# The recurrent half of the output projection as seven half-size products for eight, added to x in DRAM

## The reference, cut to what matters

```
merged = concatenate([rmsnorm(o, attn_out_g), rmsnorm(y_lru, lru_out_g)], -1)   # 512 + 512 columns
h = x + merged @ w_out                                                          # w_out 1024 x 1024
f = square(relu(rmsnorm(h, norm_mlp_g) @ w_up)) @ w_down
return h + f
```

## Time and profile before

| | us |
|---|---|
| executions, least / median / most | 2460.33 / 2461.35 / 2462.65 |
| span of the profiled execution | 2460.3 |
| TensorE busy in it | 2447.1 (99%) |
| VectorE / ScalarE / GpSimd busy | 1782.1 / 1250.7 / 517.4 |
| recurrent half of the projection, layer 0 | about 458.6 to 506.7 |
| attention half of it, layer 0 | about 506.7 to 554.4 |

### The profile page before, as it was taken

The page is one execution under the profiler, slowest core; times in us unless marked ns, Lnnn a source line. Parts: engine busy times, 40 slices in busy tenths (PEclk is TensorE's granted clock), DMA queues, the critical chain, the costliest instruction groups (busy, mean ns, idle before and its releaser), DMA issues.

```text
span 2460.3 us, 43868 instructions
## 1 busy us (share of the span) xinstructions
PE 2447.1 (99%) x17366; PEld 2361.9 (96%) x17366; DVE 1782.1 (72%) x2788; ACT 1250.7 (51%) x2237; POOL 517.4 (21%) x479
## 2 busy tenths in 40 slices
PE   9999999999999999999999999999999999999998
PEld 9999977899999999999999998779999999999998
DVE  8677767578876677677676777674887766776676
ACT  5566355435554454455525663554355544554454
POOL 0024255100112211220201142541001112111212
PEclk9999999999999999999999999999999999999999
DMA  4122201222447634764731222013135456546655
GB/s 164 52 61 73 61 11 38 90 60 102 94 86 141 125 85 99 133 120 90 218 100 52 60 74 61 11 38 98 53 115 108 88 119 132 105 88 122 131 106 181
DMA packets 104873, 230.39 MB, mean 94 GB/s; under 512 B 14896, under 2 KB 18320, under 8 KB 104672
## 3 DMA queue, kind: packets, MB, share of 16 engines
q0 software_dynamic: 43648, 89.14, 20.5%
q1 hardware_dynamic: 60880, 138.42, 17.9%
q10 hardware_dynamic: 144, 0.04, 0.0%
HBM read 144.03 MB, written 81.18 MB: 92 GB/s over the span
## 4 chain that ended last, share of the span: by engine, by line
PE 95%; DVE 2%; DMA 1%; issue 1%; ACT 0%; POOL 0%; SPq 0%; DVEq 0%; POOLq 0%; ACTq 0%
PE ps L975 28%; PE ps L1357 23%; PE ps L1406 22%; PE ps L1221 5%; PE ps L1236 4%; PE ps L1498 3%; PE ps L1291 2%; PE ps L1469 2%; PE ps L1168 2%; PE ps L1193 1%; DMA x_scratch<-stage 1%; PE ps L1099 1%; DVE mxp L2620 0%; DVE xall L2879 0%; PE ps L1004 0%
## 5 line engine op out<-in xcount | busy, mean ns | idle before, releaser
L2910 DVE TENSOR_TENSOR wlo<-raw_all,whi 128x512 fp32r<-128x512 f32 (+1 forms) x420 | 270.6, 653 | 181.3 <-ACT whi L2055 178.7
L2055 ACT ACTIVATE whi<-raw_all 128x512 fp32r<-128x512 f32 (+1 forms) x420 | 248.5, 599 | 275.4 <-PE ps L1357 85.9
L3408 POOL DMA_DIRECT2D x_scratch<-stage x224 | 199.7, 941 | 840.5 <-DVE stage L3053 695.4
L2108 ACT ACTIVATE stage<-ps 128x536 f32<-128x536 f32 (+1 forms) x224 | 135.6, 612 | 152.7 <-PE ps L1406 141.6
L3053 DVE TENSOR_TENSOR stage<-stage,ps 128x536 f32<-128x536 f32 (+1 forms) x168 | 119.0, 708 | 86.2 <-PE ps L1406 84.8
L2620 DVE TENSOR_REDUCE mxp<-ps 64x1 f32<-64x64 f32 (+11 forms) x384 | 140.4, 372 | 55.1 <-PE ps L1168 48.4
L1551 ACT ACTIVATE whi<-raw_all 128x1024 fp32r<-128x1024 f32 (+3 forms) x72 | 66.6, 925 | 199.6 <-PE ps L975 199.3
L975 PE MATMUL ps<-xgh,whi 128*128 128x358 f32 (+1 forms) x720 | 157.2, 327 | 0.0
L975 PE MATMUL ps<-xgl,whi 128*128 128x358 f32 (+1 forms) x720 | 156.7, 326 | 0.0
L975 PE MATMUL ps<-xgh,wlo 128*128 128x358 f32 (+1 forms) x720 | 156.6, 326 | 0.0
L975 PEld LDWEIGHTS ps<-xgl,whi 128*128 128x128 f32 x720 | 124.1, 189 | 0.0
(11 more groups left out here) (846 smaller groups left out, 7687.7 us busy)
## 6 DMA issues: line engine op xcount, KB each, us to landing
raw_all<-in_wst SPq DMA_DIRECT2D x233, 256.0 KB, 3.3
raw_all<-in_wst SPq DMA_DIRECT2D x78, 512.0 KB, 3.6
x_scratch<-stage POOLq DMA_DIRECT2D x112, 268.0 KB, 6.1
x_scratch<-stage POOLq DMA_DIRECT2D x112, 264.0 KB, 5.9
x_scratch<-xall POOLq DMA_DIRECT2D x24, 537.0 KB, 3.6
xall<-x_scratch SPq DMA_DIRECT2D x24, 537.0 KB, 9.7
xall<-in_xT SPq DMA_DIRECT2D x16, 537.0 KB, 6.4
raw_all<-in_wst POOLq DMA_DIRECT2D x30, 256.0 KB, 5.4
```

Source lines behind the costliest of these rows:

```text
L2055: nc.scalar.activation(dst, src, ACT.Copy).then_inc(S["u_hi"], 1)
L2108: nc.scalar.activation(quarters(stage_of(L, g, i, n)[:, 0:N2]), src, ACT.Copy, scale=-1.0 if row else 1.0).then_inc(S["x_copy"], 1)
L2910: V.tensor_tensor(dst, src, hi.bitcast(F32), ALU.subtract).then_inc(S["u_lo"], 1)
L3408: pool.dma_start(x_scr[2 * i + row, :, a:b], stage_of(L, g, i, n)[:, 0:b - a], accum_op=ALU.add).then_inc(S[done], 16)
```

## The change

The recurrent half works on four pairs of x tiles, (0,4), (1,5), (2,6), (3,7). A pair's weights are one block of 1024 columns, four blocks of two row blocks each; y is cut into feature halves and token halves. VectorE forms four sums of weight blocks in place (`y_block_sum`) and the sums of y parts (`y_first`, in attention); ScalarE and VectorE make high and low parts of four fills a pair (`y_fill_hi`, `y_fill_lo`) and of the y operands (`y_high`, `y_low`). Seven products a pair, each 2 row blocks x 3 passes x 2 pieces of 268 (264) columns. ScalarE copies four results to stages (`y_copy`), VectorE adds three (`y_add`), GpSimd issues four accumulating DMAs a pair onto x in DRAM (`y_out`), and SP then reloads x (`take_x`). In layer 0 GpSimd first copies x from the input to the DRAM scratch (`move_x`). The sum of o's squares moves behind the first unit of the attention half, and its root is made by `log_rstd`. Some semaphores are merged, without an effect on the order. The diff, without the placements of a few tables, with 16 columns of indentation taken off:

```diff
+NYP = B_OO - B_OY
+N_SPLIT = B_MLP + 3 * NYP
...
+U_Y, U_OO, U_MLP = 41, 69, 77
...
+SUM_AT = {SUM_KV: U_CQ[2], SUM_Y: U_UQ[0], SUM_Q: U_UQ[1], SUM_O: U_OO}
...
+Y_ORDER = ["P1", "P5", "P6", "P2", "P7", "P3", "P4"]
+Y_COPIES = [(0, "P1"), (0, "P5"), (0, "P6"), (1, "P1"), (0, "P4"), (1, "P5"), (1, "P6"), (2, "P1"), (1, "P4"), (2, "P5"), (2, "P6"),
+            (3, "P1"), (2, "P4"), (3, "P5"), (3, "P6"), (3, "P4")]
+Y_ADDS = ["P2", "P7", "P3"]
...
+def take_x(p):
+    for row in range(2):
+        m = OO_ORDER[2 * p + row]
+        w(f"y_out{p % 2}", 64 * (p // 2 + 1))
+        w("q_lo", NH)
+        w("pv", NH * NP)
+        sp.dma_start(x[m], x_scr[m]).then_inc(S[f"x_in{m}"], 16)
...
+y_load(3)
+take_x(0)
+w("w_lo", nth_fill(2, 3) + 2)
+sp.dma_start(raw[1][:, 0:512], wst[L * NB + B_OO, :, 0:512]).then_inc(S["raw1"], 16)
+take_x(1)
+w("w_lo", nth_fill(3, 3) + 2)
+sp.dma_start(raw[0][:, 0:512], wst[L * NB + B_OO + 1, :, 0:512]).then_inc(S["raw0"], 16)
+take_x(2)
+load(B_OO + 2)
+load(B_OO + 3)
+take_x(3)
...
+    if u in (U_OO, U_OO + 1):
+        w("y_copy", y_copied(u - U_OO + 2, "P4"))
+        w("y_add", y_added(3, "P3"))
+        return
...
+def y_product(p, name):
+    n = [name in x_ for x_ in DOWN_FILL].index(True)
+    w("w_hi", nth_fill(p, n) + 1)
+    dst = y_chain(p, L)
+    if name == "P1":
+        if p >= 2:
+            w("y_copy", y_copied(p - 2, "P4"))
+    elif name == "P5":
+        dst = y_side(L)
+        if p:
+            w("y_add", y_added(p - 1, "P3"))
+        else:
+            w("mxt", NH)
+            w("mt_lo", NH)
+    elif name == "P6":
+        w("y_copy", y_copied(p, "P1"))
+    elif name == "P2":
+        dst = pair_slot(3, L)
+        if p:
+            w("y_add", y_added(p - 1, "P2"))
+        else:
             w("o_ev", 3 * NH)
             w("s_ev", 3 * NH)
-            w("mxt", NH)
-            w("mt_lo", NH)
-        product(to_slot(U_OY[i], LIVE), U_OY[i], B_OY + bi, 512 * n, [tok(t, LIVE) for t in yh], [tok(t, LIVE) for t in yl],
-                (lambda k: w("y_lo", k + 1)) if i == 0 else None)
-        if U_OY[i] == SUM_AT[SUM_O]:
-            w("sum_lo", SUM_O)
-            sum_of_parts(SUM_O, osqt_r, osq_r)
+    elif name == "P7":
+        w("y_copy", y_copied(p, "P6"))
+    elif name == "P3":
+        dst = y_side(L)
+        w("y_copy", y_copied(p, "P5"))
+    else:
+        w("y_add", y_added(p, "P7"))
+    col0 = 256 * DOWN_FILL[n].index(name)
+    f = F_OF[name]
+    of = "b2" if f in ("b21", "b22") else f
+    opens = name in ("P1", "P5", "P2")
+    for k in range(2):
+        if p == 0:
+            w("y_hi", Y_PARTS.index((of, k)) + 1)
+        wc = slice(col0 + 128 * k, col0 + 128 * k + 128)
+        for i, (a, c) in enumerate((("h", "h"), ("l", "h"), ("h", "l"))):
+            if k == 0 and i == 1:
+                w("w_lo", nth_fill(p, n) + 2)
+            if p == 0 and c == "l":
+                w("y_made", Y_MADE.index(("lo", of, k)) + 1)
+            for t in range(2):
+                mm = nc.tensor.matmul(dst[:, t, :], ring(n + 2, whi if a == "h" else wlo)[:, wc], yop[f, k][0 if c == "h" else 1][:, t * HN:(t + 1) * HN],
+                                      start=(opens and k == 0 and i == 0), stop=(k == 1 and i == 2), skip_group_check=True)
+    mm.then_inc(S["mm"], 1)
...
+for p in range(NYP):
+    for name in Y_ORDER:
+        y_product(p, name)
 for m in range(8):
-    product(to_slot(U_OO + m, LIVE), U_OO + m, B_OO + m // 2, 512 * (m % 2), [tok(t, LIVE) for t in oh], [tok(t, LIVE) for t in ol],
+    product(to_slot(U_OO + m, LIVE), U_OO + m, *oo_block(m), [tok(t, LIVE) for t in oh], [tok(t, LIVE) for t in ol],
             (lambda k: w("o_lo", k + 1)) if m == 0 else None)
+    if m == 0:
+        w("sum_lo", SUM_O)
+        sum_of_parts(SUM_O, osqt_r, osq_r)
...
+def y_fill_hi(p, n):
+    name = f"raw{(B_OY + p) % 2}"
+    w(name, 16 * ((B_OY + p) // 2 + 1))
+    if n < 3:
+        w("yw_sum", 4 * p + (1, 2, 4)[n])
+    if p:
+        w("mm", y_done(p - 1, ("P5", "P2", "P3", "P4")[n]))
+    nc.scalar.activation(y_weights(n, whi), y_source(p, n), ACT.Copy).then_inc(S["w_hi"], 1)
...
+def y_copy(p, name):
+    n = X_COPY[name][0]
+    w("mm", y_done(p, name))
+    if p >= 2:
+        w(f"y_out{p % 2}", 64 * (p // 2))
+    src = y_side(L) if name == "P5" else y_chain(p, L)
+    nc.scalar.activation(quarters(y_stage[p % 2][n][:, 0:N2]), src, ACT.Copy).then_inc(S["y_copy"], 1)
...
+    if (h, i) == (1, 17):
+        y_fill_hi(0, 0)
+    if (h, i) == (2, 17):
+        y_fill_hi(0, 1)
+    if (h, i) == (3, 17):
+        y_fill_hi(0, 2)
+    if (h, i) == (4, 2):
+        y_fill_hi(0, 3)
+    if h == 5 and i in (6, 9):
+        y_high("t1", (6, 9).index(i))
+    if h == 6 and i in (6, 9):
+        y_high("t2", (6, 9).index(i))
+    if h == 7 and i in (2, 4):
+        y_high("b11", (2, 4).index(i))
+    if h == 7 and i in (7, 10):
+        y_high("b2", (7, 10).index(i))
+    if h == 7 and i in (13, 15):
+        y_high("t3", (13, 15).index(i))
+    if h == 7 and i in (16, 17):
+        y_high("t4", i - 16)
...
+y_copy(0, "P1")
+o_high(0)
+y_copy(0, "P5")
+y_copy(0, "P6")
+y_fill_hi(1, 0)
+o_square(0)
+y_fill_hi(1, 1)
+o_high(1)
+o_square(1)
+y_fill_hi(1, 2)
+y_copy(1, "P1")
+y_copy(0, "P4")
+y_fill_hi(1, 3)
+y_copy(1, "P5")
+y_copy(1, "P6")
+y_fill_hi(2, 0)
+o_high(2)
+y_fill_hi(2, 1)
+o_square(2)
+y_fill_hi(2, 2)
+y_copy(2, "P1")
+y_copy(1, "P4")
+y_fill_hi(2, 3)
+y_copy(2, "P5")
+y_copy(2, "P6")
+y_fill_hi(3, 0)
+y_fill_hi(3, 1)
+y_fill_hi(3, 2)
+y_copy(3, "P1")
+y_copy(2, "P4")
+y_fill_hi(3, 3)
+y_copy(3, "P5")
+y_copy(3, "P6")
 o_high(3)
 o_square(3)
-split(32)
+split(B_OO)
 w("o_sum", 3)
 nc.scalar.activation(live(osqt_r), live(osq), ACT.Copy).then_inc(S["sum_hi"], 1)
-split(33)
-root(SUM_O, rs, ATT)
-split(34)
-split(35)
+split(B_OO + 1)
+y_copy(3, "P4")
+log_rstd(SUM_O, rs, ATT)
+split(B_OO + 2)
...
+def y_block_sum(p, n):
+    a21, a22, a11, a12 = (y_blocks(p)[:, b, :] for b in range(4))
+    if n == 0:
+        w(f"raw{(B_OY + p) % 2}", 16 * ((B_OY + p) // 2 + 1))
+    else:
+        w("w_hi", nth_fill(p, (0, 1, 1)[n - 1]) + 1)
+        w("w_lo", nth_fill(p, (0, 1, 1)[n - 1]) + 2)
+        w("yw_sum", 4 * p + min(n, 2))
+    dst, a, b, op = ((a21, a21, a22, ALU.add), (a21, a21, a11, ALU.subtract), (a11, a21, a22, ALU.subtract), (a12, a12, a21, ALU.subtract))[n]
+    V.tensor_tensor(dst, a, b, op).then_inc(S["yw_sum"], 1)
...
+        if (h, i) == (4, 15):
+            y_fill_lo(0, 2)
+            y_fill_lo(0, 3)
+        if h == 4 and i in (16, 17, 18):
+            y_first(*Y_MADE[i - 16])
+        if (h, i) == (5, 0):
+            y_first("t1", 1)
+        if h == 5 and i in (15, 16):
+            y_first("t2", i - 15)
+        if h == 5 and i in (17, 18):
+            y_low("t1", i - 17)
...
+        if h == 6 and i in (15, 16):
+            y_first("t3", i - 15)
+        if h == 6 and i in (17, 18):
+            y_first("t4", i - 17)
+        if h == 7 and i in (0, 1):
+            y_low("t2", i)
+        if h == 7 and i in (3, 5):
+            y_low("b11", (3, 5).index(i))
+        if h == 7 and i in (8, 11):
+            y_low("b2", (8, 11).index(i))
+        if (h, i) == (7, 14):
+            y_low("t3", 0)
+        if (h, i) == (7, 16):
+            y_block_sum(1, 0)
...
+def y_add(p, name):
+    opened, src = {"P3": ("P6", y_side(L)), "P7": ("P5", y_chain(p, L)), "P2": ("P1", pair_slot(3, L))}[name]
+    w("mm", y_done(p, name))
+    w("y_copy", y_copied(p, opened))
+    st = quarters(y_stage[p % 2][X_COPY[opened][0]][:, 0:N2])
+    V.tensor_tensor(st, st, src, ALU.add).then_inc(S["y_add"], 1)
...
+y_low("t3", 1)
+y_low("t4", 0)
+y_low("t4", 1)
 o_low(0)
-add_y(0)
+y_fill_lo(1, 0)
+y_block_sum(1, 1)
+y_add(0, "P2")
+y_add(0, "P7")
+y_fill_lo(1, 1)
+y_block_sum(1, 2)
+y_block_sum(1, 3)
+y_add(0, "P3")
+invert(3)
+y_fill_lo(1, 2)
 o_low(1)
-invert(3)
+y_block_sum(2, 0)
+y_fill_lo(1, 3)
+y_fill_lo(2, 0)
+y_block_sum(2, 1)
+y_add(1, "P2")
+y_add(1, "P7")
+y_fill_lo(2, 1)
+y_block_sum(2, 2)
+y_block_sum(2, 3)
+y_add(1, "P3")
+y_fill_lo(2, 2)
 o_low(2)
-add_y(1)
-split(31)
-add_y(2)
+y_block_sum(3, 0)
+y_fill_lo(2, 3)
+y_fill_lo(3, 0)
+y_block_sum(3, 1)
+y_add(2, "P2")
+y_add(2, "P7")
+y_fill_lo(3, 1)
+y_block_sum(3, 2)
+y_block_sum(3, 3)
+y_add(2, "P3")
+y_fill_lo(3, 2)
 divide(3)
-add_y(3)
+y_fill_lo(3, 3)
 o_low(3)
-split(32)
+y_add(3, "P2")
+split(B_OO)
+y_add(3, "P7")
 sum_lo(osq_r, osq, osqt_r, SUM_O)
-add_y(4)
-split(33)
-add_y(5)
-add_y(6)
-split(34)
-rstd(rs, SUM_O)
-add_y(7)
-split(35)
+y_add(3, "P3")
+split(B_OO + 1)
+w("rstd", SUM_O)
...
+    pool.dma_start(x_scr[m], xT[m]).then_inc(S["x_out"], 16)
 for c in range(3):
     cube(c)
+    if L == 0:
+        move_x(2 * c)
+        move_x(2 * c + 1)
+if L == 0:
+    move_x(6)
+    move_x(7)
...
+def y_out(p, name):
+    n, row, h = X_COPY[name]
+    if name == "P4":
+        w("y_copy", y_copied(p, "P4"))
+    else:
+        w("y_add", y_added(p, {"P1": "P2", "P5": "P7", "P6": "P3"}[name]))
```

(60 more changed lines are left out.)

214 lines of the change are left out of this document (115 added, 99 removed).

## The result

The changed kernel takes **2473.18 us** (median of 5 executions, 2470.68 to 2474.08), the kernel before, run beside it, 2460.33 us: ratio **1.0051**, 95% interval 1.0040 to 1.0062, +12.9 us. The forecast was 2465.0, between 2454 and 2471; slower was right, the size was not.

What follows compares the result with a forecast made beforehand. TensorE, busy all the time, was taken as the bound: 11.1 us saved on matmuls, against 7.0 us of gaps and 0.35 of attention phase per layer, gave +3.6 us on 2461.35, so 2465.0 us, range 2454 to 2471.

Steps and rivals of the forecast that it cites:

- What bounds the kernel, and the price of a matmul: TensorE always busy; 288 recurrent matmuls a layer become 336 at 123.95 ns in layer 0, gross gain 11.1 us.
- Step 1, P4 of pair 0: Recurrent half: P4 waits for VectorE's add of P7, queued behind the low part of o0; gap 1.55 us a layer.
- Step 2, P4 of pair 3: Recurrent half: adds queue behind the low part of o3, slowed by GpSimd's add; gap 3.6 us, 1.7 without the collision.
- Step 3: First attention-half product waits for the add of P3 of pair 3, behind a low part; gap 0.35 us a layer.
- Step 4: Third attention-half product waits for the moved sum of squares, its root and the first scaling; gap 1.5 us a layer.
- drain: Skill page's 1.38 us per table switch at the root; would make the fourth gap 2.9, total 2.8 us higher; not counted.
- Attention phase: Attention heads before the recurrent half take in the preparation work: +0.35 us a layer, bounds -0.5 and +1.5.
- The copy of x to DRAM: Eight GpSimd-issued transfers in layer 0's first projections could delay weight loads: cost 0, upper end 3 us.
- rival of head phase and loads: Attention phase and layer 0's weight loads at their upper ends: 2470 us, chance 0.10.
- Landings: Rival: late accumulates delay ScalarE's copies of pairs 2 and 3, +2.3 us a layer, 2469.6 us; chance 0.18.
- The queues keep up: Rival: no P4 stops in the recurrent half, only the two attention-half gaps stay; 2454.6 us, chance 0.22.
- The signs of being wrong: P4 stops absent or under 1 us, ScalarE awaiting DMA before pair 2's first copy, or heads over 1 us longer.

Runs made afterwards that it cites:

- Experiment 2: Changed kernel with GpSimd's three adds of o's squares cut from full width to 8 columns; 2463.73 us, 1.0016 of the kernel before.
- experiment 1: Changed kernel with VectorE's low part of o0 moved behind the adds of P2 and P7 of pair 0; 2472.06 us, 1.0050 of the kernel before.
- experiment 6: Changed kernel with VectorE's product adds ahead of its low parts and block sums, and ScalarE's P1 copies of pairs 1 and 2 ahead of a fill; 2463.22 us, 1.0012.
- Experiment 10: Kernel before with one TensorE wait added: each layer's first recurrent product waits for the low part of o0, 4.2 us; 2472.42 us, 1.0049.
- experiment 3: Changed kernel with pair 3's adds of P2, P7 and P3 ahead of the low part of o3, the squares' sum's low part behind; 2465.97 us, 1.0028.
- experiment 7: Changed kernel with VectorE's adds ahead of its SBUF work, and the third attention block's load and split earlier; 2455.06 us, 0.9978 of the kernel before.
- experiment 4: Changed kernel with VectorE's adds reordered in pairs 0, 1 and 3, and the third attention block's split ahead of the root; 2474.52 us, 1.0054.
- experiment 5: Changed kernel with attention-block loads ahead of x tiles on SyncE and the third block's split ahead of the root; 2469.36 us, 1.0037 of the kernel before.

## Why the forecast was wrong, step by step

*What bounds the kernel, and the price of a matmul:* right. P5 of pair 2 to P4 of pair 3's wait, 144 matmuls from 486.44 to 504.50, is 125 ns each for the forecast 123.95. The saving is 0.3 us a layer less than forecast.

*Step 1, P4 of pair 0:* right in place and cause, 1.9 for 1.55. Experiment 2, which leaves it, and experiments 1 and 6, which reorder the queue and remove it, show that it is the queue's order.

*Step 2, P4 of pair 3:* right, 3.7 for 3.6, with the low part at 3.20 beside GpSimd. "Without the collision 1.7" came out as 1.69 in experiment 2.

*The step that failed, a stop left out of the sum:* "By that rule GpSimd's other two adds delay fills of pairs 1 and 2 too; what changes with it is only slack." I had the rule and did not walk it through the queue. GpSimd's second add of squares met the two block sums of pair 2, which grew by 2.7 us, and the add behind them made P5 of pair 2 late by 1.35 and 1.5 us. Experiment 2 removes this stop. VectorE's work with two SBUF inputs grew in every trace in which it met a full-width add of GpSimd that had started first or with it: 3.20, 2.60 and 2.17 us for 1.34, 0.76 and 0.68, and 3.47 for 0.76 where the add came between the two block sums; not one add with a PSUM input grew beside it (0.70 to 0.71). That is the rule of the page "SBUF — State Buffer", Who interferes with whom, of the Trainium skill, as the forecast has it. Where VectorE came first, GpSimd's add grew as well: the one from 482.39 took 2.65 us for 2.09.

*The second step that failed, a term that was absent:* the clock. I read 1.00 in every window of a kernel without stops and priced each new stop at its length. It was 3.2 us in layer 0 and 1.7 in layer 1, the largest part of what the forecast misses. Experiment 10 shows it, and experiment 3 agrees: its span is 7.8 us shorter, of which the shorter stops before P4 of pair 3 are only 3.6. Three slow stretches are gone with it, two of them behind those stops; the third, behind P4 of pair 0 in layer 0, is gone though its stop of 1.73 us is unchanged. Together the two steps are 2.9 + 4.9 = 7.8 us. The forecast's +3.6 us and the +11.1 of the spans differ by 7.5; the smaller terms of the account nearly cancel.

*Step 3:* no stop for 0.35: P4 of pair 3, at half clock, ended at 510.3, after the add (509.9). *Step 4:* right, 1.5; no drain appears: the table load starts 0.02 us after the logarithm's last part ends. ScalarE, changed kernel:

```profile
519.53 0.29 ACT L1766 ACTIVATE rs<-ps,eps 128x50 f32<-128x50 f32 x1
519.84 1.28 ACT L1768 ACT_TABLE_LOAD   x1
521.13 1.10 ACT L1768 ACTIVATE rs<-rs 128x1074 f32<-128x1074 f32 x1
```

*Attention phase:* 0.3 and 0.5 for 0.35, within its bounds. The copy of x to DRAM, issued from 100.6 to 156.0 us, cost nothing: layer 0's projections take 254.5 us in both (31.85 to 286.35, and 32.28 to 286.76). So the rival of head phase and loads did not decide.

*Landings:* ScalarE waited for no accumulate in the recurrent half of either layer, so this rival did not decide. But the cover that I named was thin. The accumulates of the recurrent half land in a median 7.6 us for the 6.0 of the earlier trace rows. With the stops removed ScalarE does wait for them (4.2 us in experiment 6, 3.9 in experiment 7, at one copy), and the weight load behind the x tiles is late: the third attention product stopped for up to 5.9 us (experiments 4 and 6). *The queues keep up* falls with the stops at the recurrent product.

The signs of being wrong that I had named did not come: both P4 stops are there, ScalarE waits for no accumulate, and the heads take less than 1 us more in all. The length of the recurrent half did speak against the sum, 51.4 us for 46.8.

## What to carry to other kernels

When a full TensorE is given fewer matmuls, price each new stop twice: its length, and the slow matmuls behind it, some 1.7 us here. All stops of 3.5 us or more had them, and three of 21 between 1.6 and 2.2 us; the lengths between were not seen. Walk every GpSimd instruction that reads SBUF against VectorE's queue, not only those seen to collide before; if it can't be moved, put what TensorE waits for (adds with a PSUM input) ahead of work with two SBUF inputs. A repaired stop is judged only with the next one mended too: experiment 1 gained nothing, since the collision moved to the next product, experiment 4 lost and experiment 6 gave back part of its gain, both until the load in SyncE's queue was moved.

## What was not expected of the hardware

A stop of 1.75 us costs 1.7 us, one of 4.2 costs 6.0 (half of +3.3 and of +12.0, which are known to within 2.2 and 3.4 us). Among stops of 1.6 to 2.2 us the clock fell in 3 of 21, in the same program in one layer and not in the other (1.73 us idle in layer 0 of the changed kernel, 1.75 in layer 1), and behind the same stop of 1.73 us at P4 of pair 0 in the changed kernel and not in experiments 2, 3 and 5, so that a profile of one execution can't settle this term. A load of 256 KB, 3.3 us by its median over the kernel, took 8.2 us in layer 1, where accumulates and x tiles shared the DMA engines with it. In layer 0, from 478 to 500 us, these engines are 0.98 busy for 0.19 in the kernel before.
